# Four Y units of a hybrid layer as 512-column products, their two halves added on VectorE

## The reference, cut to what matters

```python
h = rms_norm(x, mix_norm_g[layer])
proj = h @ w_in[layer]
xr, yg, q, k, v = jnp.split(proj, splits, axis=-1)      # five parts of 512 columns
...
y_lru = rg_lru(xr, ...) * jax.nn.gelu(yg.astype(jnp.float32))
...
mixed = jnp.concatenate([rms_norm(y_lru, lru_out_g[layer]), rms_norm(y_attn, attn_out_g[layer])], axis=-1)
x = x + mixed @ w_out[layer]
```

## Time and profile before

| | |
|---|---|
| median of 3 runs | 290.15 us (289.98 to 290.15) |
| the profiled execution's own time | 290.13 us |
| its span, first to last instruction | 288.4 us |
| busy: TensorE, VectorE, ScalarE | 284.1, 244.2, 202.9 us |
| mean granted TensorE clock | 1.000 |

### The profile page before, as it was taken

The page is one execution under the profiler, slowest core; times in us unless marked ns, Lnnn a source line. Parts: engine busy times, 40 slices in busy tenths (PEclk is TensorE's granted clock), DMA queues, the critical chain, the costliest instruction groups (busy, mean ns, idle before and its releaser), DMA issues.

```text
span 288.4 us, 5012 instructions
## 1 busy us (share of the span) xinstructions
PE 284.1 (99%) x1642; PEld 246.6 (86%) x1642; DVE 244.2 (85%) x448; ACT 202.9 (70%) x389; POOL 11.4 (4%) x26
## 2 busy tenths in 40 slices
PE   8999999999999999999999999999999999999996
PEld 7688999898788999888888888888888888888885
DVE  2998898889999888999988788888888888888765
ACT  4893599999897687778676766667666666676540
POOL 3000004600000000000000000000000000000000
PEclk9999999999999999999999999999999999999999
DMA  7999950440365705375647474544647454100003
GB/s 276 428 419 419 398 186 7 148 145 14 134 228 209 257 38 164 130 291 166 278 145 287 148 261 177 160 162 152 252 145 291 145 181 178 77 0 0 0 0 145
DMA packets 8111, 52.23 MB, mean 181 GB/s; under 512 B 928, under 2 KB 1312, under 8 KB 2080
## 3 DMA queue, kind: packets, MB, share of 16 engines
q1 hardware_dynamic: 7920, 51.50, 48.1%
q0 software_dynamic: 176, 0.53, 0.5%
HBM read 50.98 MB, written 1.05 MB: 180 GB/s over the span
## 4 chain that ended last, share of the span: by engine, by line
PE 95%; DMA 2%; DVE 1%; ACT 1%; SPq 0%; issue 0%
PE bank L1419 25%; PE bank L1062 15%; PE bank L1063 14%; PE bank L1066 14%; PE bank L1423 13%; PE bank L1118 3%; PE bank L1372 3%; DMA x_tok<-in_x_dram 2%; PE bank L1383 1%; PE bank L1182 1%; PE bank L1306 1%; PE bank L1213 1%; PE bank L1222 1%; PE bank L1339 1%; PE bank L1176 1%; DVE w_hi L691 0%
## 5 line engine op out<-in xcount | busy, mean ns | idle before, releaser
L703 DVE TENSOR_TENSOR w_lo<-raw,w_hi 128x1024 fp32r<-128x1024 f32 x93 | 110.9, 1221 | 4.5 <-ACT w_hi L381 3.9
L381 ACT ACTIVATE w_hi<-raw 128x1024 fp32r<-128x1024 f32 x83 | 84.2, 1058 | 2.3 <-PE bank L1066 1.9
L1419 PE MATMUL bank<-h_both,w_hi 128*128 128x512 f32 x320 | 79.6, 391 | 0.0
L1419 PEld LDWEIGHTS bank<-h_both,w_hi 128*128 128x128 f32 x320 | 58.8, 188 | 11.3
L1423 PEld LDWEIGHTS bank<-h_both,w_lo 128*128 128x128 f32 x320 | 43.7, 191 | 3.1
L1423 PE MATMUL bank<-h_both,w_lo 128*128 128x256 f32 x320 | 44.7, 283 | 0.0
L614 ACT ACTIVATE tanh_a<-bank 128x256 f32<-128x256 f32 x44 | 16.7, 381 | 38.7 <-PE bank L1423 38.7
L1063 PE MATMUL bank<-w_lo,act_hi 128*128 128x512 f32 (+1 forms) x90 | 34.9, 388 | 0.0
L1062 PE MATMUL bank<-w_hi,act_hi 128*128 128x512 f32 (+1 forms) x90 | 34.9, 388 | 0.0
L1066 PE MATMUL bank<-w_hi,act_lo 128*128 128x512 f32 (+1 forms) x90 | 34.6, 385 | 0.0
L622 ACT ACTIVATE xc<-ygate,par 128x256 f32<-128x256 f32 x44 | 26.2, 596 | 4.2 <-DVE ygate L985 4.2
(11 more groups left out here) (193 smaller groups left out, 411.4 us busy)
## 6 DMA issues: line engine op xcount, KB each, us to landing
raw<-in_stream_dram SPq DMA_DIRECT2D x47, 1024.0 KB, 4.8
x_tok<-in_x_dram SPq DMA_DIRECT2D x2, 512.0 KB, 5.0
out_dram<-x_tok SPq DMA_DIRECT2D x3, 256.0 KB, 2.1
p_T<-in_gates_dram POOLq DMA_DIRECT2D x1, 512.0 KB, 9.5
out_dram<-x_tok SPq DMA_DIRECT2D x2, 128.0 KB, 2.0
par<-in_params_dram SPq DMA_DIRECT2D x1, 117.0 KB, 6.6
mix_g<-in_params_dram POOLq DMA_DIRECT2D x1, 4.0 KB, 5.6
```

The lines of the kernel that those rows point to most:

```text
L381: act.activation(hi_tile(u)[:, :], raw_unit(u), ACT.Copy).then_inc(hi_done, 1)
L703: dve.tensor_tensor(w_lo[u % RING][:, :], raw_unit(u), hi_tile(u)[:, :].bitcast(F32), ALU.subtract).then_inc(lo_done, 1)
L1419: pe.matmul(acc[:, :], whi[:, kc, :], h_both[:, kc, :, :].rearrange("p b t -> p (b t)"), start=kc == 0, stop=False)
```

## The change

The four Y units take the form of the FFN's. Each gets a bank of its own in turn (2, 3, 2, 3): eight products of 512 columns put high weights by high h in the first half and high weights by low h in the second, then, after the wait for the low weights, eight products of 256 columns add to the first half. A new VectorE instruction for each unit, `y_join`, reduces over the two halves, reading column t of the first and column t of the second in turn, straight from PSUM, and writes 256 columns to `ygate` in SBUF. The GELU then reads and writes `ygate`. The third and fourth unit wait until the bank's earlier reduction is done. The four reductions stand in VectorE's order where the diff shows them.

```diff
-        Y_ACC, V_ACC = bank[2:4], bank[4:6]
+        Y_SIDES, V_ACC = bank[2:4], bank[4:6]
...
             for j in range(2):
-                act.wait_ge(unit_used, U_Y + 2 * j + 2)
-                act.activation(ygate[:, 2 * j:2 * j + 2, :], Y_ACC[j][:, :].rearrange("p (c t) -> p c t", c=2),
+                act.wait_ge(y_joined, 2 * j + 2)
+                act.activation(ygate[:, 2 * j:2 * j + 2, :], ygate[:, 2 * j:2 * j + 2, :],
                                ACT.Gelu_apprx_tanh).then_inc(ygate_done, 1)
...
+            def y_join(c):
+                dve.wait_ge(unit_used, U_Y + c + 1)
+                dve.tensor_reduce(ygate[:, c, :], Y_SIDES[c % 2][:, :].rearrange("p (b t) -> p t b", b=2), AX_X,
+                                  ALU.add).then_inc(y_joined, 1)
+
...
             row_reciprocals(2)
+            y_join(0)
             los(15, 16)
...
             dve.tensor_scalar(log_c, lam_p, -LRU_C, None, ALU.mult).then_inc(log_c_done, 1)
+            y_join(1)
             shift(4)
...
             los(17, 18)
             hi(20)
+            y_join(2)
+            y_join(3)
 
             dve.wait_ge(a2_done, 1)
...
             def y_unit(c):
-                cols_unit(U_Y + c, Y_ACC[c // 2][:, SEQ * (c % 2):SEQ * (c % 2 + 1)])
+                u = U_Y + c
+                whi, wlo, acc = by_chunk(w_hi[u % RING]), by_chunk(w_lo[u % RING]), Y_SIDES[c % 2]
+                if c >= 2:
+                    pe.wait_ge(y_joined, c - 1)
+                pe.wait_ge(hi_done, hi_count(u))
+                for kc in range(KC):
+                    pe.matmul(acc[:, :], whi[:, kc, :], h_both[:, kc, :, :].rearrange("p b t -> p (b t)"),
+                              start=kc == 0, stop=False)
+                split(u)
+                for kc in range(KC):
+                    ins = pe.matmul(acc[:, 0:SEQ], wlo[:, kc, :], h_hi[:, kc, :], start=False, stop=kc == KC - 1)
+                ins.then_inc(unit_used, 1)
```

More of the change, by code:

```diff
@@ L207, in build_layer @@
         lru_in, scan_done = sem("lru_in"), sem("scan_done")
+        y_joined = sem("y_joined")
         ygate_done, y_done, y_sq_done, y_chunks = sem("ygate_done"), sem("y_done"), sem("y_sq_done"), sem("y_chunks")
```

## The result

The changed kernel takes **290.91 us** (290.80 to 291.02, 10 runs), the kernel before, run beside it, 290.12 (289.98 to 290.16, 10 runs). The ratio is 1.0030, 95% interval 1.0022 to 1.0038: slower by 0.8 us, where 290.9 was forecast. The profiled execution took 290.98 us for a span of 289.2; before it was 290.13 and 288.4.

What follows compares the result with a forecast made beforehand. TensorE, busy 99% of the span, was taken as the bound; VectorE's lateness would hold it 0.79 us back at unit 27, the products' 0.36 gain already contained: 290.13 + 0.79 = 290.9 us, range 290.1 to 292.8.

Steps and rivals of the forecast that it cites:

- The products: On TensorE, each of the four Y units takes 2.79 us instead of 2.88, a gain of 0.36 us in all.
- The reduction: Four new VectorE reductions of 512 PSUM elements occupy 0.60 us each; bounds 0.34 and 1.13.
- R: Time that one reduction occupies VectorE, taken as 0.60 us.
- Where they sit: Reductions' places in VectorE's order: starts at 49.28, 55.62 and 63.92 us, leaving VectorE 0.91 us late from 65.12.
- D: VectorE's lateness behind the fourth reduction, 4 R - 1.49, forecast as 0.91 us.
- The deadlines: VectorE outputs hold TensorE late: last head's probabilities 0.41 us, mix_lo 0.57, unit 27's low half 0.79; the largest stands.
- What costs nothing: TensorE's waits for the first two reductions, later splits, scores' shift, log_c, GELU and reloads are covered, by about a microsecond.
- The jump costs: Rival: the reduction's 256-element hops cost extra, R towards 1.13, time 292.0 to 293.0 us; chance 0.30.
- VectorE's slack covers the reductions: Rival: VectorE's idle time hides the reductions if R is under 0.40, and the 0.36 gain shows, 289.8 us; chance 0.12.
- rule for unit 27: TensorE is late at the output projection's last unit by VectorE's lateness less 0.12 us, forecast as 0.79.
- TensorE needs VectorE's dense stretch less tightly than I read: Rival: mix_lo, not unit 27's load, has the last word, 0.57 us late, 290.7; forecast's low side, 0.15 of its 0.58.

Runs made afterwards that it cites:

- experiment 2: Changed kernel with the old 24 products of 256 columns, into the first half of the bank, reductions kept: 291.07 us.
- experiment 5: Changed kernel with split of unit 27 earlier, then conversion of unit 22, conversion of unit 21 and first reduction later, added in turn: 290.69, 290.43, 290.47, 290.11 us.
- experiment 4: Changed kernel with each reduction reading its 512 elements in order, summing neighbours instead of the two halves: 290.86 us.
- experiment 3: Changed kernel with each reduction replaced by a copy of the first half, 256 elements: 289.99 us.
- Experiments 1: Kernel before with the new products and no reductions: 290.07 us; with VectorE's split of unit 27 also moved earlier: 289.87 us.
- all_moves: Changed kernel with VectorE's split of unit 27 moved earlier, and conversions of units 22 and 21 and the first reduction moved later: 290.11 us.
- all_norm: Changed kernel with the four moves of all_moves, and VectorE's splits of units 28 and 29 also moved later: 289.75 us.

## Why the prediction was right

Time and mechanism came as forecast. That the time was met to 0.01 us is luck: single steps were off by 0.04 to 0.09, and in part they cancel. The steps one by one:

- *The products.* Forecast 0.36 in all, measured about 0.30: a Y unit takes 0.07 to 0.09 less. Its length was read short on both sides of the change: unit 12 takes 2.97 before (2.88 forecast, from 24 steps of 0.12) and 2.88 after (2.79, from the FFN). That this gain would not show, because it is contained in places that VectorE sets, is borne out by experiment 2: without it the FFN comes later by VectorE's 0.20 and not by the 0.31.
- *The reduction.* R = 0.60 forecast, 0.60 measured, 0.69 in duration against 0.682 to 0.691. The Trainium skill's Vector Engine (DVE) Microarchitecture Reference, section 5.2 Measured stream behaviour on trn2, gave two readings for SBUF, a hop at every element that costs and two regions in turn at the full rate. Out of PSUM this trace agrees with the second: 686 ns with the jump, 683 without.
- *Where they sit.* First reduction 49.30 (forecast 49.28), second 55.60 (55.62), last two 63.88 (63.92), line 872 at 65.08 (65.12): D = 0.87 for 0.91.
- *The deadlines.* Probabilities 0.32 late (forecast 0.41), mix_lo 0.62 (0.57), unit 27 0.75 past its first product (0.79); FFN 0.78. That the largest of them counts and not their sum is shown by experiment 5: each of the first two that are taken away uncovers the next, and behind the third mix_lo is missed again. The forecast had only the last head's probabilities; the trace has a wait for the head before it as well.
- *What costs nothing.* TensorE does not stand at units 14 and 15: unit 15 runs at 59.72, its bank's reduction is through at 56.29. VectorE's lag ends at the residual, where it stands 0.27 for TensorE in front of 100.06. The residual's first piece itself starts 1.12 late (95.64 for 94.52) and not 0.8: ahead of it VectorE stands 0.34 for which the profile names no releaser. The transposes behind it are 0.78 late all the same.
- *The jump costs* fell with experiment 4. *VectorE's slack covers the reductions* fell with R, but experiment 3 shows its condition met: with R near 0.37 nothing is lost. Its price was off, and this was a slip of reasoning: it let the whole 0.36 come out at 289.8, while the prediction's own rule for unit 27 (D - 0.12) allows TensorE to be only 0.12 early when D is 0. Experiments 1 and 3, 290.07 and 289.99, sit there.
- *TensorE needs VectorE's dense stretch less tightly than I read* fell by a little: unit 27 adds 0.13 to the 0.62 of mix_lo. With that split moved, the kernel takes the 290.7 that this rival named (290.69).

What the prediction lacked is a fourth deadline: the residual and norm chain on VectorE, which it let shift with the rest and never priced by itself. It did not show in the changed kernel, where the transposes keep their 5.19; it decided as soon as the three were gone. The piece of all_moves that was left, V 16 to FFN 51.16 for 50.90, is that 0.23 between the transposes and 0.03 not traced; all_norm, which moves only units 28 and 29 further, takes away both.

## What to carry to other kernels

When work is put on an engine beside the path, list every output that the bound engine takes from it afterwards, with the slack of each: here the loss was the largest excess, not the sum, and removing one deadline bought only the step down to the next. A deadline that is met can be missed again once the bound engine gets there earlier. A gain on the bound engine is held back by the same list, since an engine that gets early meets the smallest slack; so a reordering that does nothing by itself can be what lets the gain out. In VectorE's list, a conversion whose reader is far off belongs behind the small result that is wanted next.

## What the runs showed of the hardware

A VectorE reduction out of PSUM that takes its elements in turn from two places 256 fp32 columns apart costs the same as one in order: 686 against 683 ns for 512 elements. And a weight load that comes late shows mostly in the product behind it: the load of unit 27 waited 0.29, TensorE was 0.62 late before it and 0.64 at its first product, but that product took 0.50 us, where its like took 0.39, and the products after it are 0.75 late. Of the 0.29, TensorE lost 0.13.
